# Decoder trunk step: gate logits computed in half tiles inside the prompt's softmax attention and kept in DRAM, expert slot table built on chip

## What is computed

```
h = rms_norm(x) * (1 + scale1) + shift1            # 544 tokens x 1024
z = h @ w_in                                        # q, k, v | forget logits | 3 x 1024 gate columns
gates = sigmoid(z[..., 3 * MIX_WIDTH + 6:]).reshape(b, s, 3, 1024)
...                                                 # three attention mixers give o_sb, o_dil, o_fox
merged = gates[:, :, 0] * (o_sb @ w_br_sb) + gates[:, :, 1] * (o_dil @ w_br_dil) \
       + gates[:, :, 2] * (o_fox @ w_br_fox)
x = x + gate1 * (merged @ w_o)
h2 = rms_norm(x) * (1 + scale2) + shift2
...                                                 # top group, two of its four experts, for each token
x = x + gate2 * sum over the two experts of (silu(h2 @ w1) * (h2 @ w3) * gate) @ w2
```

## Time and profile before

| | us |
|---|---|
| median of 3 runs | 1601.27 |
| lowest, highest | 1600.67, 1602.63 |
| profiled execution | 1605.7 |
| its span, first to last instruction | 1604.0 |
| PE busy in the span | 1308.8 (82%) |
| DVE, ACT, POOL busy | 451.3, 276.1, 172.1 |
| moved by DMA | 290.94 MB |

### The profile page before, as it was taken

The page is one execution under the profiler, slowest core; times in us unless marked ns, Lnnn a source line. Parts: engine busy times, 40 slices in busy tenths (PEclk is TensorE's granted clock), DMA queues, the critical chain, the costliest instruction groups (busy, mean ns, idle before and its releaser), DMA issues.

```text
span 1604.0 us, 20181 instructions
## 1 busy us (share of the span) xinstructions
PE 1308.8 (82%) x6971; PEld 849.5 (53%) x6971; DVE 451.3 (28%) x1156; ACT 276.1 (17%) x565; POOL 172.1 (11%) x242
## 2 busy tenths in 40 slices
PE   4699998657998568888877699999993499999990
PEld 2377775533455445555555488888443244444440
DVE  3200000754344234444444211111243011111116
ACT  2201011322222122222222000000110011111112
POOL 0000000501223100000000000000001211121110
PEclk9799999677557778899999699999995699999995
DMA  9622340378000398889987741111011899999934
GB/s 313 242 105 106 107 166 35 104 251 299 1 0 1 97 313 291 261 267 293 299 292 261 266 137 53 53 53 53 4 43 21 256 341 318 307 309 328 316 128 167
DMA packets 145446, 290.94 MB, mean 181 GB/s; under 512 B 16350, under 2 KB 67239, under 8 KB 144288
## 3 DMA queue, kind: packets, MB, share of 16 engines
q1 hardware_dynamic: 135584, 268.18, 50.0%
q0 software_dynamic: 9792, 21.89, 3.8%
HBM read 276.73 MB, written 43.38 MB: 200 GB/s over the span
## 4 chain that ended last, share of the span: by engine, by line
PE 74%; DVE 10%; issue 6%; DMA 4%; POOL 2%; SPq 2%; ACT 2%; DVEq 0%; POOLq 0%; ACTq 0%
PE psum L825 64%; PE psum L1097 5%; DVE arena L1686 2%; DMA wring<-in_w_mod 2%; PE psum L1026 2%; POOL wring L749 2%; PE psum L1136 1%; DVE wring L1694 1%; DVE hT L2250 1%; DVE wring L1686 1%; PE psum L954 1%; DVE arena L1694 1%; DVE xT L2057 1%; POOL expert_slots L777 1%; DVE arena L697 1%
## 5 line engine op out<-in xcount | busy, mean ns | idle before, releaser
L825 PE MATMUL psum<-hT,wring 128*128 128x272 f32 x1536 | 360.7, 395 | 8.3 <-ACT hT L1419 8.3
L825 PEld LDWEIGHTS psum<-hT,wring 128*128 128x128 f32 x1536 | 293.6, 192 | 73.9 <-issue 12.9
L825 PE MATMUL psum<-arena 128*8 128x128 f32 (+6 forms) x1488 | 248.5, 370 | 5.9 <-DVE arena L1686 3.5
L825 PE MATMUL psum<-wring,hT 128*128 128x512 f32 x384 | 173.4, 605 | 18.9 <-DVE hT L2250 16.8
L825 PEld LDWEIGHTS psum<-arena 128*8 128x8 f32 (+5 forms) x1488 | 131.8, 135 | 100.4 <-issue 83.9
L825 PE MATMUL psum<-wring,arena 128*8 128x128 f32 (+3 forms) x1008 | 119.7, 417 | 14.6 <-DMA wring<-in_w_mod 8.4
L825 PEld LDWEIGHTS psum<-wring,hT 128*128 128x128 f32 x384 | 71.9, 192 | 106.4 <-issue 103.5
L1686 DVE TENSOR_TENSOR arena<-arena,psum 128x544 f32<-128x544 f32 (+8 forms) x79 | 32.1, 431 | 217.7 <-ACT arena L1419 201.1
L1419 ACT ACTIVATE arena<-psum 128x544 f32<-128x544 f32 (+1 forms) x48 | 24.1, 503 | 400.3 <-PE psum L825 400.3
L825 PEld LDWEIGHTS psum<-wring,arena 128*8 128x8 f32 (+3 forms) x1008 | 52.0, 111 | 70.3 <-issue 58.9
L825 PE MATMUL psum<-arena,small 128*128 128x256 f32 (+8 forms) x162 | 51.6, 444 | 38.4 <-DVE arena L1686 26.4
(11 more groups left out here) (235 smaller groups left out, 1167.4 us busy)
## 6 DMA issues: line engine op xcount, KB each, us to landing
wring<-in_w SPq DMA_DIRECT2D x48, 1024.0 KB, 11.4
arena<-in_cache_kv SPq DMA_DIRECT2D x128, 320.0 KB, 3.5
wring<-in_w_mod SPq DMA_DIRECT2D x12, 2048.0 KB, 14.0
wring<-in_w_in SPq DMA_DIRECT2D x12, 2048.0 KB, 11.8
arena<-in_w SPq DMA_DIRECT2D x24, 1024.0 KB, 5.2
xT<-in_cache_kv SPq DMA_DIRECT2D x64, 320.0 KB, 3.6
wring<-in_cache_kv SPq DMA_DIRECT2D x64, 320.0 KB, 3.5
out_dil_sample<-in_cache_dil SPq DMA_DIRECT2D x8, 2044.0 KB, 37.5
```

The lines of the kernel that those rows point to most:

```text
L825: return T.matmul(out, lhsT, rhs, start=start, stop=stop, **k)
```

## The change

The 24 gate tiles are cut into 48 half tiles (8 matmuls on 272 tokens). PE does them in the attention stage, one in each even unit and two in each odd unit (`FILL`, `gate_unit`), into banks 6 and 7. ACT copies each, without the sigmoid, to `gate_st`, which is `xT` (`gate_out`); SP stores four tiles at a time to `gate_tiles` in DRAM. The gate weights come in twelve chunks of 1 MB through three buffers, `gate_w`. To free the banks, all six `fox_rows` go before the first unit, through banks 2 to 7, and `nck` keeps all six.

In the branch stage PE does the branch products alone, with four pairs of banks. The raw logits come back in five loads of up to five tiles through two buffers, `gate_in`; ACT takes the sigmoid from there. Both output weight chunks and the whole tail are issued in one go, after the second of these loads and ahead of the third.

The output rows of a tile are done in two halves with turned rows between, and DVE and ACT take their steps in another order. The slot table comes from ten matmuls of a one-hot matrix of slots with the payloads (24 chunks x 3 values), so the scatters, the load-back and the filling at the start go. POOL's loop over chunks is written out, and it takes row numbers straight from the table.

```diff
+        gate_d = nc.dram_tensor("gate_tiles", [P, 24, TOK], F32, kind="Internal").ap()
+        nck = [flat_ring[:, a:a + SEQ] for a in (0, 512, 1024, 1536, 11008, 11520)]
+        GATES = 24
+        STAGE, TURN = 4, 5
+        gate_st = xT
+        FILL = [(3 * n // 2 + n % 2,) if n % 2 == 0 else (3 * n // 2, 3 * n // 2 + 1) for n in range(NU)]
...
+            sp.wait_ge(sem("st_k"), 16 * KV_STORES)
+            for c in range(GATES // 2):
+                if c == 1:
+                    sp.wait_ge(sem("sbo_mm"), 4)
+                if c >= 3:
+                    sp.wait_ge(sem("gate_mm"), 4 * (c - 2))
+                sp.dma_start(gate_w[c % 3], wi[:, 3078 + 256 * c:3334 + 256 * c].rearrange("(k p) n -> p k n", p=P)
+                             ).then_inc(sem(f"ld_w{c % 3}"), 16)
+                if c >= 4 and c % 2 == 0:
+                    gate_store(c // 2 - 2)
+            gate_store(4)
+            gate_store(5)
...
+            for n in range(2):
+                sp.wait_ge(sem(f"st_g{n}"), 16 * 3)
+            gate_load(0)
...
+            sp.wait_ge(sem("seq_pv"), NB)
+            sp.wait_ge(sem("seq_out"), NB)
+            gate_load(1)
             for half in range(2):
...
+                chunk(30 + half, half, wo[:, 512 * half:512 * half + 512])
...
+            for n in range(2, 5):
+                sp.wait_ge(sem("gate_ev"), 2 * GATES + TURN * (n - 1))
+                gate_load(n)
...
-            def fox_rows(h):
-
-                if h >= 2:
-                    pe.wait_ge(sem("nck_ev"), h - 1)
-                mm(banks[6 + h % 2], pick_head[0:NFOX, 128 * h:128 * h + 128], ncumT[0:NFOX, 0:SEQ]
+            for h in range(NFOX):
+                mm(banks[2 + h], pick_head[0:NFOX, 128 * h:128 * h + 128], ncumT[0:NFOX, 0:SEQ]
                    ).then_inc(sem("nck_mm"), 1)
+
+            def gate_unit(u):
+
+                t, half = u // 2, u % 2
+                c = t // 2
+                if u % 4 == 0:
+                    pe.wait_ge(sem(f"ld_w{c % 3}"), 16 * (6 + c // 3 + 1))
+                if u >= 2:
+                    pe.wait_ge(sem("gate_ev"), u - 1)
+                for k in range(KD):
+                    last = mm(banks[6 + half][:, 0:HALF], gate_w[c % 3][:, k, 128 * (t % 2):128 * (t % 2) + 128],
+                              hT[:, k, HALF * half:HALF * half + HALF], k == 0, k == KD - 1)
+                last.then_inc(sem("gate_mm"), 1)
...
+            pe.wait_ge(sem("nck_ev"), NFOX)
             for n in range(NU):
-                if n % 4 == 0 and n // 4 + 1 < NFOX:
-                    fox_rows(n // 4 + 1)
                 if n + 2 < NU:
                     scores(n + 2)
+                gate_unit(FILL[n][0])
                 turn_weights(n)
+                for u in FILL[n][1:]:
+                    gate_unit(u)
                 if n:
                     weigh(n - 1)
...
+            for n in range(GATES):
+                b, m = n // KD, n % KD
+                if n >= 4:
+                    pe.wait_ge(sem("br_ev"), n - 3)
+                kts = ((0, 1), (2,), (3, 4, 5))[b]
+                for k in kts:
+                    last = mm_tokens(2 * (n % 4), wbr[:, k, 128 * m:128 * m + 128], oT[:, k, :], k == kts[0], k == kts[-1])
+                last.then_inc(sem("gate_mm"), 1)
...
+            pe.wait_ge(*done_at("onehot_ready"))
+            for n in range(10):
+                r = rows_of(n // TOP)
+                last = mm(banks[7][:, 0:3 * CHUNKS], slot_oh[0:r, n, :], pay_c[0:r, n, :], n == 0, n == 9)
             last.then_inc(sem("routing"), 1)
...
-                f(as_halves(gsig[:, n % 2, :]), halves(2 * (n % 2)), ACT.Sigmoid).then_inc(sem("gate_ev"), 1)
+                f(gsig[:, n % 2, :], gate_in[n // TURN % 2][:, n % TURN, :], ACT.Sigmoid).then_inc(sem("gate_ev"), 1)
...
-            for k in range(TOP):
-                link(tt(r_sel, r_a[:, k], r_sb, ALU.mult))
-                link(V.tensor_reduce(r_dest[:, :, k], r_sel, AX, ALU.add))
-            V.tensor_copy(dest_i, r_dest.rearrange("p i k -> p (i k)")).then_inc(sem("routing"), 1)
...
+            tt(slot_oh, row_ids.unsqueeze(1).to_broadcast([P, 10, P]), r_s.unsqueeze(2).to_broadcast([P, 10, P]),
+               ALU.is_equal)
...
+            dve.wait_ge(*done_at("slots_mm"))
+            slots = banks[7][:, 0:3 * CHUNKS].rearrange("p (c j) -> p c j", j=3)
+            V.tensor_copy(tok_i, slots[:, :, 0])
```

More of the change, by code:

```diff
@@ L601, in _ @@
[L601 to L604, removed]
-            sp.wait_ge(sem("gate_mm"), 24)
+                chunk(30 + half, half, wo[:, 512 * half:512 * half + 512])
+            sp.wait_ge(sem("st_modrows"), 128)
+            sp.dma_start(g_rows, mod_d[0:1, :].to_broadcast([P, 4 * D])
+                         .rearrange("p (s d) -> p s d", d=D)).then_inc(sem("ld_tail"), 16)
@@ L813, in _, with settle @@
-            for c in range(RING):
-                gather(0, c, c)
-            with pool.Fori(0, CHUNKS // RING - 1) as i:
-                for u in range(RING):
-                    gather(i, RING + u, u)
-                    scatter(i, u, u)
-            for u in range(RING):
-                scatter(0, CHUNKS - RING + u, u)
+            pool.wait_ge(*done_at("slots_ready"))
+            def settle():
+                link(nc.gpsimd.tensor_tensor(carried[0:1, :], ones[0:1, 0:1], ones[0:1, 0:1], ALU.mult))
@@ L822, in _ @@
+            settle()
+            for c in range(CHUNKS + RING):
+                if c < CHUNKS:
+                    gather(c)
+                if c >= RING:
+                    scatter(c - RING)
         @block.tensor
@@ L1278, in _, with out_rows @@
             pe.wait_ge(sem("br_ev"), 24)
-            def out_rows(i):
-                if i >= 2:
+            def out_rows(i, half):
+                if i >= 2 and not half:
                     pe.wait_ge(sem("xo_ev"), i)
-                for half in range(2):
-                    for k in range(KD):
-                        last = mm(banks[2 * (i % 2) + half], merged[:, k, 128 * i:128 * i + 128], wo_part(half, k),
-                                  k == 0, k == KD - 1)
-                last.then_inc(sem("xo_mm"), 1)
+                for k in range(KD):
+                    last = mm(banks[2 * (i % 2) + half], merged[:, k, 128 * i:128 * i + 128], wo_part(half, k),
+                              k == 0, k == KD - 1)
+                if half:
+                    last.then_inc(sem("xo_mm"), 1)
             def out_rows_sample():
@@ L2103, in _ @@
                 stage(0, NB - 1)
-            for n in range(24):
-                half, b, j = n // 12, (n // 4) % 3, n % 4
-                m = 4 * half + j
-                dve.wait_ge(sem("gate_ev"), n + 1)
+            for n in range(GATES):
+                b, m = n // KD, n % KD
+                dve.wait_ge(sem("gate_ev"), 2 * GATES + n + 1)
+                dve.wait_ge(sem("gate_mm"), 2 * GATES + n + 1)
                 out = merged[:, m, :] if b == 0 else btmp[:, n % 2, :]
-                last = tt(as_halves(out), as_halves(gsig[:, n % 2, :]), halves(4 + 2 * (n % 2)), ALU.mult)
+                last = tt(as_halves(out), as_halves(gsig[:, n % 2, :]), halves(2 * (n % 4)), ALU.mult)
                 if b:
```

274 lines of the change are left out of this document (131 added, 143 removed).

## The result

The changed kernel takes 1550.68 us (median of 4 runs, 1547.90 to 1555.62), against 1601.95 for the kernel before in the same comparison: a ratio of 0.967, 95% interval 0.962 to 0.972. The forecast was 1551. The profiled execution of after took 1555.6 us, the longest of the four, and its span is 1553.6; before's span was 1604.0.

A forecast was written before the change was run, and what follows sets the result against it. TensorE was taken to bound all long stages, at half clock in much of attention. Attention +130, branch -158, output rows -8 and routing -14 gave -50; 1605.7 - 50 - 4.4 = 1551 us, range 1523 to 1583.

The forecast's parts named there:

- What bounds the kernel, and what a busy microsecond is worth: Whole kernel: TensorE is busy in all long stages, but at clock 0.60 in attention and 0.98 in the branch stage.
- Attention stage, +130: Attention stage: grows from 157 to 287 us by taking in the gate matmuls; bounds +110 to +160.
- Own work, seams and slow clock: Attention stage: its own matmuls 86 us, 48 starts of gate half tiles 7, lower clock after the pause 3.
- The bound of 80: Attention stage: lower limit of 80 us for its own work if all busy time scales with the clock.
- The new wait, 13: Attention stage start: PE stands 13 us for first gate weights, queued on SP behind the cache-shift copies; they land near 400.5.
- Branch stage, -158: Branch stage: gate matmuls gone, but PE waits some 20 us for logits behind SP's tail loads; bounds -182 to -148.
- Rival 1: Branch stage: the tail doesn't hold the gate tiles, so it ends 15 to 22 us earlier, about 1531; chance 0.17.
- Output rows, -8: Output rows and logits: earlier turns leave about 13 us after the last matmul; 8 us saved, bounds -12 to -3.
- routing, -14: Routing: slot table by small matmuls replaces scatters and load-back, first turn at 1249.7, not 1263.9; bounds -17 to -9.
- Dear seams: Attention stage: own work 100 us, each start 0.25; +20, about 1571; chance 0.22 shared with PE stopping for ACT's copies.
- Copies of ACT that stop PE: Attention stage: PE stops at gate banks, POOL waits stay; 15 us more; chance 0.22 shared with costlier half-tile starts.
- The falling clock: Attention stage: clock falls in every piece of attention work, own columns cost 66 us more, 1617; chance 0.08.

The follow-up runs named there:

- The clump: Changed kernel with all 48 gate half tiles in one run after the last attention unit, none between units; 1598.68 us, ratio to before 0.995.
- the second profile: Profile of the changed kernel run once more, unedited; 1549.05 us median of 6 runs.
- 4 of 8 feature tiles: Changed kernel with half of the gate product left out of each gate half tile; attention stage 198.4 us, one execution.
- 1 of 8: Changed kernel with seven eighths of the gate product left out of each half tile; attention stage 147.1 us, or 141.1 with first gate weights loaded ahead of cache-shift copies.
- the second comparison: Changed kernel, unedited, timed again beside the follow-up kernels against the kernel before; 1549.05 us, ratio 0.963.

## Why the prediction was right

**What bounds the kernel, and what a busy microsecond is worth.** Right, and it is the step that carried the forecast. A count of records alone (177.6 us out of one stage, 177.6 into another) gives no gain. The clump comes near that count made real: 1598.7 us, and what it gains comes from the output rows and the routing.

**Attention stage, +130 (measured +125.4 and, in the second profile, +127.6).** Own work, seams and slow clock were put at 86 + 7 + 3 = 96; measured 91.0 with all three in it. A stretch of gate work costs some 0.2 us in the run with the cut half tiles (forecast 0.15), so 48 are some 10, and some 81 are left where 89 stood. The bound of 80 (all busy time scales with the clock) was nearer than I took it: by the gate records' rate, the columns of the mixed run of 26 records need 4.4 us of its 5.09, 0.17 us a record and not 0.15, so I put the part that does not scale too high. Seams too cheap and own work too dear partly made up for each other. POOL's 15.2 us went as said.

**The new wait, 13 (measured 13.5).** Cause and size are right. Both ends were 3.4 us off in the same direction: PE reached the wait at 390.4, not 387, because the six broadcasts and first scores took 10.5 us at the lower clock, and the load landed near 403.9, not 400.5. The run with the early load shows that the whole wait came from the load's place behind the copies.

**Branch stage, -158 (-161.5 and -159.3).** The chain was ACT waiting for load 2, DVE for ACT, PE for DVE: 19.7 us on PE (21.4 in the second profile), some 20 forecast. The 192 branch records took 46.9 us at a clock of 0.97, where 44.4 had been taken from the gate records' rate. The load was issued 33.7 us after the stage began; 36 was forecast. Rival 1 (the tail doesn't hold the loads: 1531) is what POOL's queue brings about: 1529.45. The order on SP decided; the two runs that moved the first load of weights and loads 2 to 4 of the logits agree, with 11.4 and 19.6 us. The Trainium skill's page DMA: Bandwidth & Descriptors, section "Queues, rings and completion order", which the forecast drew on, says that each DMA engine consumes descriptors in ring order. The trace agrees for the first wait: 59.0 us from issue to landing behind the copies, 5.4 ahead of them. For the second wait the forecast leaned on that rule wrongly, though its sum did not: the load landed 5.9 us after its issue, and what made PE wait was that SP, held by w_re, had not issued it.

**Output rows, -8 (-7.0), and routing, -14 (-14.6).** As forecast. DVE was done with the payload matrix 9.6 us after the start of the rank matmuls, where 9.9 had been summed; the 20 small records took 4.75 us, 4.5 summed:

```profile
1195.73 1.15 PE L841 MATMUL psum<-arena,small 128*128 128x80 f32 x4 [5.55 <-DVE arena L2244]
1205.38 4.75 PE L841 MATMUL psum<-arena,wring 128*128 128x72 f32 x20 [8.50 <-DVE arena L1720]
1215.83 1.97 PE L1388 MATMUL psum<-small,oT 128*128 128x128 f32 x8 [5.70 <-DMA oT<-expert_in_rows,arena]
```

**The rivals.** Dear seams: some 0.2 us measured, midway between the forecast's 0.15 and this rival's 0.25, but the own work that it put at 100 us is some 81. Copies of ACT that stop PE: in the changed kernel PE never waits for them. The falling clock (8%): it had for it that PE was busy for 92% of a stretch at 0.50, and against it that the dilated units ran at 1.00. The runs show that it would not have come about with far less gate work either. The form of the rival was wrong: I let the clock fall within each piece of attention work, but with 8 or 4 of 8 feature tiles it held 1.00 from 440 us to the end of the stage. With 1 of 8 it did dip, as to 0.50 from 490 to 492 us.

**What was not in the sum.** The sample stage moved by +10.4 us in the first profile and by -1.4 in the second, with nothing changed in it. The forecast's terms were 4.6 us too high (attention), 3.5 too low in gain (branch), and 3 us were gained at the ends. That the total met the median to 0.3 us is therefore partly luck: over the executions seen, a sum of stages is good to some 5 us here. In the second comparison, with eleven runs of before, the gain is 59 us where 50 was forecast, and its interval (0.959 to 0.967) leaves out the forecast's ratio of 0.969.

## What to carry over

Before moving work between stages, read the granted clock of both, not only the busy time: 768 records cost 125 us inside a stage that had run at 0.60, a wait of 13.5 included, and 176 behind the same stage. A small share of the work is enough for that (a quarter of it brought the own work to 101 us, all of it to 91), so if only part can be moved, move part, and put it between the small matmuls. Then look what stands ahead of each new load on its queue: both waits that this change made were for loads of 1 to 1.4 MB that stood behind others in SP's program, and two edits of the order gave back 32 of the 33 us.

## What was not expected of the hardware

- TensorE at 1.00 with less work: with 1 of 8 feature tiles and the early load PE was busy 71.7 of 80 us at clock 1.00, in the clump 105.7 of 115 at 0.50. The share of busy time in a trace does not tell the clock; what stood between did. Why two gate records per half tile suffice, where the units' own matmuls and transposes do not, is open: no other kind of filler was tried.
- A pause of 16 us with the same matmuls behind it left the clock at 0.50, and the stage was 20 us longer.
- The issue of w_re, 64 byte rows, held SP 16.1 us, and 25.4 us when POOL's loads ran beside it. Two loads of 1 MB held it 21.9 us in after, at a time when the DMA engines were busy for 0.96 of the stretch from 380 to 404 us:

```profile
379.27 21.87 SPq L523 DMA_DIRECT2D wring<-in_w_in  x2
```

  While one issue is held, whatever is next in that engine's program waits. Why it is held is not shown.
- The same sample stage took 352.1 to 365.2 us in different executions, at granted clocks of 0.90 to 0.85; no other stage varied so.
